# Normed expert results written as rows by indirect DMA, in a two-layer decoder step with grouped MoE

## The reference

```
x <- LN(a*x + mixer(x))                      # HGRN2 in layer 0, GLA in layer 1
x <- LN(a*x + memory_cross_attention(x))
x <- LN(a*x + grouped_moe(x))                # a = (2*DEPTH)**0.25
```

```
h = silu(x @ w_gate[e]) * (x @ w_up[e])      # 1024 -> 512
y = y + combine[..., e:e+1] * (h @ w_down[e])
mu = mean(z); var = mean((z - mu)**2); z = (z - mu) * rsqrt(var + 1e-5) * g + b
```

## Time and profile before

| what | us |
| --- | --- |
| median of 3 runs (1395.2 to 1398.28) | 1397.25 |
| the profiled execution | 1396.09 |
| its span | 1394.3 |
| PE busy / DVE / ACT / POOL | 1346.6 / 1023.6 / 756.0 / 140.6 |

### The profile page before, as it was taken

One profiled execution on the slowest core, in us unless ns is written; L12 is line 12 of the kernel. 1 busy time (PEld: TensorE's weight loads), 2 busy tenths in 40 slices (PEclk: granted clock), 3 DMA queues, 4 the chain that ended last, 5 costly groups with the idle time before them and its releaser, 6 DMA issues.

```text
span 1394.3 us, 19745 instructions
## 1 busy us (share of the span) xinstructions
PE 1346.6 (97%) x7689; PEld 1118.5 (80%) x7689; DVE 1023.6 (73%) x1102; ACT 756.0 (54%) x775; POOL 140.6 (10%) x209
## 2 busy tenths in 40 slices
PE   8999999999898999999999999999899999999996
PEld 6898997788676888888887798779777788888884
DVE  4456757773578988898887256782558889898986
ACT  4445624423425876767676353332434777677765
POOL 5200246100000000000000015200000000000000
PEclk9999999999999999999999999999999999999998
DMA  9774545437954999999994455444983799999981
GB/s 284 258 256 151 166 154 145 127 122 261 370 228 154 363 360 337 354 349 351 338 357 146 130 192 171 133 150 170 375 318 143 276 366 340 350 345 338 363 319 38
DMA packets 102002, 353.67 MB, mean 254 GB/s; under 512 B 6368, under 2 KB 32496, under 8 KB 72224
## 3 DMA queue, kind: packets, MB, share of 16 engines
q1 hardware_dynamic: 97056, 336.09, 67.0%
q0 software_dynamic: 4864, 16.45, 3.5%
HBM read 332.85 MB, written 19.67 MB: 253 GB/s over the span
## 4 chain that ended last, share of the span: by engine, by line
PE 80%; DVE 10%; ACT 4%; DMA 3%; issue 1%; SPq 1%; DVEq 0%; ACTq 0%
PE ps L1883 65%; DMA att_kt<-in_cache_mem_v 2%; PE ps L2253 1%; DMA raw<-in_xattn_w_kv 1%; PE ps L2463 1%; PE ps L2276 1%; DVE mix_s L1594 1%; PE ps L2264 1%; PE ps L1892 1%; DVE x L1314 1%; PE ps L1891 1%; DVE x L1311 1%; PE ps L1993 1%; DVE x L1277 1%; DVE stats L1290 1%
## 5 line engine op out<-in xcount | busy, mean ns | idle before, releaser
L1247 DVE TENSOR_TENSOR w_lo<-raw,w_hi 128x2048 fp32r<-128x2048 f32 x64 | 146.0, 2293 | 125.9 <-ACT w_hi L827 125.8
L1883 PE MATMUL ps<-w_hi,xt_hi 128*128 128x512 f32 x576 | 229.6, 399 | 5.9 <-DVE w_lo L1251 2.2
L1883 PE MATMUL ps<-w_hi,xt_lo 128*128 128x512 f32 x576 | 225.5, 392 | 0.0
L1883 PE MATMUL ps<-w_lo,xt_hi 128*128 128x512 f32 x512 | 200.4, 392 | 0.0
L827 ACT ACTIVATE w_hi<-raw 128x2048 fp32r<-128x2048 f32 x64 | 121.7, 1913 | 141.8 <-PE ps L1883 64.6
L1251 DVE TENSOR_TENSOR moe_lo<-moe_in_raw,w_hi 128x2048 fp32r<-128x2048 f32 x72 | 164.2, 2290 | 22.6 <-ACT w_hi L834 22.6
L1251 DVE TENSOR_TENSOR w_lo<-raw,w_hi 128x2048 fp32r<-128x2048 f32 x72 | 164.8, 2291 | 16.7 <-ACT w_hi L834 16.2
L834 ACT ACTIVATE w_hi<-moe_in_raw 128x2048 fp32r<-128x2048 f32 x72 | 138.1, 1918 | 56.5 <-PE ps L1883 56.5
L834 ACT ACTIVATE w_hi<-raw 128x2048 fp32r<-128x2048 f32 x72 | 137.5, 1913 | 14.8 <-PE ps L1883 14.8
L1883 PE MATMUL ps<-xt_hi,w_hi 128*128 128x320 f32 x448 | 138.7, 310 | 0.2
L1883 PE MATMUL ps<-xt_lo,w_hi 128*128 128x320 f32 x448 | 138.4, 309 | 0.0
(11 more groups left out here) (407 smaller groups left out, 2573.0 us busy)
## 6 DMA issues: line engine op xcount, KB each, us to landing
raw<-in_moe_w_gate SPq DMA_DIRECT2D x48, 1024.0 KB, 5.2
moe_in_raw<-in_moe_w_down SPq DMA_DIRECT2D x48, 1024.0 KB, 4.9
moe_in_raw<-in_moe_w_up SPq DMA_DIRECT2D x32, 1024.0 KB, 5.7
raw<-in_moe_w_up SPq DMA_DIRECT2D x32, 1024.0 KB, 5.9
raw<-in_hgrn_w_in SPq DMA_DIRECT2D x16, 1024.0 KB, 5.6
raw<-in_cache_mem_k SPq DMA_DIRECT2D x16, 1024.0 KB, 6.3
moe_in_raw<-in_moe_w_gate SPq DMA_DIRECT2D x16, 1024.0 KB, 6.1
raw<-in_moe_w_down SPq DMA_DIRECT2D x16, 1024.0 KB, 5.0
```

The lines of the kernel that those rows point to most:

```text
L1247: nc.vector.tensor_tensor(lo_at(slot_of(k)), raw_at(slot_of(k)), hi_at(hi_slot(k)).bitcast(F32), ALU.subtract).then_inc(w_low, 1)
L1883: ins = mm(out, lhs, rhs, start=start and n == 0, stop=stop and n == 2, skip_group_check=shared)
```

## The change

The result of a visit stays in slot order. `row_sum` (DVE) adds a times the gathered input (`xa`, a copy of `xg` made by POOL) to the sums in PSUM, at the start of the next visit. ACT makes the row sums at j = 1 (`row_sums`) and, at j = 8, loads the table with Ln and Exp, computes 1/sqrt(var), and loads silu's table again (`row_rstd`). DVE does the two passes of the norm at j = 8 and j = 10 (`row_gain`, `row_norm`). POOL writes the 128 rows to the table `x_next[l]` in DRAM by an indirect DMA (`scatter`), with row numbers `row_out`; slots without a token go to row 0, which nobody reads. `s`, `pt`, `y_hi`, `y_lo`, `pick_t`, the scaling of x in visit 0, `tile_sums` and `tile_scale` go. `pick` of the next visit is made at DVE's j = 14, `ix` comes behind chunk 15, and in visit 0 a task `own` (j = 5) makes the row numbers of that visit. Between the layers SP loads x from `x_next[0]` and PE turns it behind three half blocks of the memory projection; at the end SP copies `x_next[1]` to the outputs. The diff, cut:

```diff
-SIDE = {1: ("s", 0), 3: ("s", 1), 5: ("s", 2), 7: ("s", 3), 9: ("s", 4), 11: ("s", 5),
-        12: ("pt", 0), 14: ("ix", 0), 20: ("t", 0), 21: ("t", 1)}
+SIDE = {5: ("own", 0), 15: ("ix", 0), 20: ("t", 0), 21: ("t", 1)}
...
     n = KT // len(X_AFTER)
     return range(X_AFTER.index(db) * n, X_AFTER.index(db) * n + n) if db in X_AFTER else ()
+def norms(q):
+    return TILES * (q - q // 3)
 def ln_loaded(q):
...
...
         for part in range(2):
             sp.wait_ge(mem_in[part], 32)
             sp.dma_start(late_mem[part].bitcast(F32), mem_rows_kept[part]).then_inc(mem_in[part], 16)
+    if l == 1:
+        dense(done, done + NR + 2, groups)
+        sp.wait_ge(mo[0]["out"], groups * 16)
+        for t in range(TILES):
+            sp.dma_start(x[0:live(t), t, :], x_next[0][1 + t * P:1 + t * P + live(t), :]).then_inc(x_in, 16)
+        done += NR + 2
     dense(done, in_end(l), groups)
     sp.wait_ge(mx_scan, 8 * l + H)
...
...
         group(l, last, i if groups is None else groups + i, i % GROUPS, False)
     group(l, last, nl if groups is None else groups + nl, GROUPS - 1, False)
     groups = nl + 1 if groups is None else groups + nl + 1
-for t in range(TILES):
-    sp.wait_ge(ln_done, TILES * (3 * LAYERS - 1) + t + 1)
-    rows = a["y_prompt"][0, t * P:(t + 1) * P, :] if t < 2 else a["y_sample"].rearrange("b t c -> (b t) c")
-    sp.dma_start(rows, x[0:live(t), t, :]).then_inc(y_out, 16)
-sp.wait_ge(y_out, 16 * TILES)
+sp.wait_ge(mo[1]["out"], nl * 16 + 16)
+sp.dma_start(a["y_prompt"][0], x_next[1][1:1 + PROMPT, :]).then_inc(y_out, 16)
+sp.dma_start(a["y_sample"].rearrange("b t c -> (b t) c"), x_next[1][1 + PROMPT:1 + NT, :]).then_inc(y_out, 16)
+sp.wait_ge(y_out, 32)
 for par in range(2):
...
...
     def gather(i):
-        pool.wait_ge(s["read"], side_start(i) + (3 if isinstance(i, int) else 9))
+        pool.wait_ge(s["read"], side_start(i) + (3 if isinstance(i, int) else 2))
+        pool.wait_ge(s["xa"], i + 1)
         nc.gpsimd.sem_inc(x_go, 1)
         nc.gpsimd.indirect_dma_start(st_moe["xg"][:], None, x_rows_out[l][:, :],
                                      bass.IndirectOffsetOnAxis(ap=row_ix[:, 0:1], axis=0)).then_inc(s["xg_in"], 16)
+    def keep_rows(i):
+        if isinstance(i, int):
+            pool.wait_ge(s["read"], 2)
+        else:
+            pool.wait_ge(s["read"], side_start(i))
+            pool.wait_ge(s["z"], i * 3)
+        nc.gpsimd.sem_inc(x_go, 1)
+        nc.gpsimd.tensor_copy(st_moe["xa"][:], st_moe["xg"][:]).then_inc(s["xa"], 1)
+    def scatter(i):
+        pool.wait_ge(s["z"], i * 3 + 2)
+        nc.gpsimd.sem_inc(x_go, 1)
+        nc.gpsimd.indirect_dma_start(x_next[l][:, :], bass.IndirectOffsetOnAxis(ap=row_out[:, 0:1], axis=0),
+                                     x[:, 1, :], None).then_inc(s["out"], 16)
+    keep_rows(0)
     gather(0)
     pool.wait_ge(rt_n, l + 1)
     nl = pool.value_load(n_last[0:1, 0:1], min_val=3, max_val=11)
     with pool.Fori(1, nl) as i:
+        keep_rows(i)
+        scatter(i)
         gather(i)
+    keep_rows(nl)
+    scatter(nl)
+    scatter(nl + 1)
...
-    def sums_out(g):
-        act.wait_ge(w_used, at(base, g, GCH))
-        nc.scalar.activation(m["y_hi"][:].rearrange("p (a c) -> p a c", a=2), ps[:, 4:6, :], ACT.Copy).then_inc(s["yh"], 1)
+    def row_sums(i):
+        act.wait_ge(s["z"], i * 3)
+        nc.scalar.activation(m["aside"][:], x[:, 0, :], ACT.Copy, scale=-1.0 / D, accum_out=mean_var[:, 0, 0:1]).then_inc(s["zs"], 1)
+        act.wait_ge(s["zs"], i * 4)
+        nc.scalar.activation(m["aside"][:], x[:, 0, :], ACT.Square, bias=mean_var[:, 0, 0:1], accum_out=mean_var[:, 0, 1:2]).then_inc(s["zs"], 1)
+    def row_rstd(i):
+        act.wait_ge(s["zs"], i * 4 + 1)
+        nc.scalar.activation(rstd[:, 0:1], mean_var[:, 0, 1:2], ACT.Ln, bias=ln_eps[:, 0:1], scale=1.0 / D).then_inc(s["zs"], 1)
+        act.wait_ge(s["zs"], i * 4 + 2)
+        nc.scalar.activation(rstd[:, 0:1], rstd[:, 0:1], ACT.Exp, scale=-0.5).then_inc(s["zs"], 1)
     def visit(i, first, last_one):
         g = i if groups is None else groups + i
-        if not first:
-            sums_out(g)
         uses = side_order(first, last_one)
...
             for e in range(EPG):
...
             for k, (jj, what, n) in enumerate(uses):
                 if max(jj, 0) == j:
                     side(i, what, n, side_start(i) + k + 1)
-            if first and 4 <= j < 4 + TILES:
-                act.wait_ge(s["xl"], TILES)
-                act.wait_ge(ln_in, rows_kept(l))
-                nc.scalar.activation(x[:, j - 4, :], x[:, j - 4, :], ACT.Copy, scale=ALPHA).then_inc(s["scaled"], 1)
             if j + MH < GCH or not last_one:
                 split_expert(l, j + MH, g, False)
             elif l == 0 and j + MH - GCH < NH:
                 split_next(j + MH - GCH, g)
+            if not first and j == 1:
+                row_sums(i)
+            if not first and j == 8:
+                nc.scalar.preload_act_table_set("natural_log_exp_and_others")
+                row_rstd(i)
+                nc.scalar.preload_act_table_set("silu_and_others")
     for k, (what, n, bank) in enumerate((("g", 0, 7), ("g", 1, 6), ("t", 0, 2), ("t", 1, 3))):
-        side(0, what, n, SKIPPED + k + 1, bank)
+        side(0, what, n, k + 1, bank)
     base = CHUNKS0 if l == 0 else CHUNKS1
     visit(0, True, False)
...
...
         visit(i, False, False)
     visit(nl, False, True)
     groups = nl + 1 if groups is None else groups + nl + 1
-    sums_out(groups)
+    nc.scalar.preload_act_table_set("natural_log_exp_and_others")
+    row_sums(nl + 1)
+    row_rstd(nl + 1)
     def kv_block_out(db):
         par = db % 2
         block_out(db, groups, kv_staged(db), ps[:, 4 * par:4 * par + 2, :], ACT.Copy).then_inc(evac[par], 1)
...
-    def sums_out(i):
-        dve.wait_ge(s["yh"], i)
-        V_.tensor_tensor(m["y_lo"][:].rearrange("p (a c) -> p a c", a=2), ps[:, 4:6, :],
-                         m["y_hi"][:].rearrange("p (a c) -> p a c", a=2).bitcast(F32), ALU.subtract).then_inc(s["yl"], 1)
+    def rows_taken(i):
+        if not isinstance(i, int):
+            dve.wait_ge(s["out"], i * 16)
+        V_.tensor_copy(row_out[:], row_ix[:])
+    def next_pick(i, first):
+        dve.wait_ge(s["side"], side_start(i) + (2 if first else 1))
+        dve.wait_ge(s["p"], i * 2 + 2)
+        for t in range(TILES):
+            ins = V_.tensor_scalar(m["pick"][:, t, :], slot_no[:], u_slot[:, t:t + 1], None, ALU.is_equal)
+        ins.then_inc(s["p"], 1)
+        dve.wait_ge(s["p"], i * 2 + 3)
+        V_.tensor_scalar(u_slot[:], u_slot[:], -float(P), None, ALU.add).then_inc(s["p"], 1)
+    def row_sum(i, g):
+        dve.wait_ge(w_used, at(base, g, GCH))
+        dve.wait_ge(s["xa"], i)
+        V_.scalar_tensor_tensor(out=x[:, 0, :].rearrange("p (a c) -> p a c", a=2), in0=m["xa"][:].rearrange("p (a c) -> p a c", a=2),
+                                scalar=ALPHA, in1=ps[:, 4:6, :], op0=ALU.mult, op1=ALU.add).then_inc(s["z"], 1)
+    def row_gain(i):
+        dve.wait_ge(s["zs"], i * 4)
+        V_.scalar_tensor_tensor(out=x[:, 1, :], in0=x[:, 0, :], scalar=mean_var[:, 0, 0:1], in1=ln_gb[:, 0, :],
+                                op0=ALU.add, op1=ALU.mult).then_inc(s["z"], 1)
+    def row_norm(i):
+        dve.wait_ge(s["zs"], i * 4 + 3)
+        dve.wait_ge(s["z"], i * 3 + 1)
+        V_.scalar_tensor_tensor(out=x[:, 1, :], in0=x[:, 1, :], scalar=rstd[:, 0:1], in1=ln_gb[:, 1, :],
+                                op0=ALU.mult, op1=ALU.add).then_inc(s["z"], 1)
     def visit(i, first, last_one):
         g = i if groups is None else groups + i
         if not first:
-            sums_out(i)
+            row_sum(i, g)
         uses = side_order(first, last_one)
         for j in range(GCH):
             for e in range(EPG):
...
                 V_.tensor_tensor(m["ht_lo"][:, e % 2], ps[:, 6, :].rearrange("p (k s) -> p k s", k=4),
                                  m["ht_hi"][:, e % 2].bitcast(F32), ALU.subtract).then_inc(s["htl"], 1)
             for k, (jj, what, n) in enumerate(uses):
-                if max(jj, 0) == j and not (what == "pt" and last_one):
+                if max(jj, 0) == j:
                     side(i, what, n, side_start(i) + k + 1)
+            if j == PICK_AFTER:
+                rows_taken(i)
+                if not last_one:
+                    next_pick(i, first)
             if j + MH < GCH or not last_one:
                 split_expert(base + j + MH, j + MH, g)
             elif l == 0 and j + MH - GCH < NH:
                 split_next(j + MH - GCH, g)
+            if not first and j in NORM_AFTER:
+                (row_gain, row_norm)[NORM_AFTER.index(j)](i)
     split_expert(base + 1, 1, g0)
     for n in range(2):
-        side(-1, "t", n, SKIPPED + 3 + n, 2 + n)
+        side(-1, "t", n, 3 + n, 2 + n)
     link(V_.tensor_reduce(m["gm"][:], m["sel"][:], AX_X, ALU.max))
     first_of(m["r2"][:], m["sel"][:], m["gm"][:], e_rank[:], EXPERTS)
...
```

(64 more changed lines are left out.)

95 lines of the change are left out of this document (24 added, 71 removed).

## The result

The changed kernel takes 1403.29 us (median of 17 runs, 1396.24 to 1410.26) against 1396.98 for the kernel before on the same chip (17 runs, 1395.13 to 1398.37). The ratio is 1.0041, 95% interval 1.0026 to 1.0055: slower by 0.4%, where 1391.0 was forecast, and 1.3 us past the range's upper end. The runs lie 14 us apart where those of before lie 3 apart.

A forecast was written before the change was run, and what follows sets the result against it. TensorE, busy 97% of the span, was taken as the bound. Layers -6.0, between them -1.5 and tail +1.0 sum to -6.5 us, from the median of 1397.25 to 1390.75, say 1391; range 1384 to 1402.

The forecast's parts named there:

- PE's work removed: Each visit but the first: TensorE loses six row sums (2.8 us) and pick's transposes (0.33), together 3.13 us.
- The first visit: First visit of a layer: net +0.35 us of PE work and 0.2 late, +0.55 in all.
- The table switch: ScalarE at j = 8: two table loads, 1.30 us per switch without a drain; 3.1 us with Ln and Exp.
- Rival 2: ScalarE at j = 8: a table switch costs double, load plus drain; PE waits 5.5 us four times; 1404; chance 0.05.
- The place and mean size of the stall: Visits 1 and 2 of both layers: PE waits 2.9 us ahead of "ix", as DVE's pick queues behind the scatter.
- Rival 1: rows_taken in visits 1 and 2: scatter lands late, change slower from about 10 us; 1407 at 11; chance 0.16.
- What a stall costs: Visits 1 and 2 of a layer: only the wait charged, -3.13 + 2.92 = -0.2 us each.
- Last visits: Last visit of a layer: no pick, no "ix", scatter wait hidden up to a landing near 9.8; keeps -3.13 us.
- Between the layers: Stretch to the dense blocks: they start at 28.3 us against 30.2, -1.9, of which -1.5 is kept.
- The tail: End of the kernel: scatter lands in 6.0 us, then DRAM-to-DRAM copy; 19.3 us against 18.28, +1.0.
- Rival 4: Tail: DRAM to DRAM at half the rate, +5 us rather than +1; 1395; chance 0.24 including a landing near 9.4.
- rival 3: Visits: scatter lands by 6.0 us, DVE's own queue sets a stall of 1.6; -13 us, 1384; chance 0.10.

The follow-up runs named there:

- the run of 1399.17: Profiled run of the changed kernel in the main measurement, unaltered; 1399.17 us, where the median of 17 runs is 1403.29.
- the run of 1412.95: Changed kernel measured again, unaltered; its profiled and longest run, 1412.95 us; median of 9 runs 1405.82, ratio 1.0056 against the kernel before.

## Why the prediction was wrong

- **PE's work removed**, 3.13 us a visit: right, 3.28 measured in undisturbed visits. The first visit: +0.44 in both layers, forecast +0.55.
- **The table switch**: right. The load ends where Ln starts and the next begins 0.02 behind Exp, as ScalarE's timeline of after has it:

```profile
542.48 1.28 ACT L1233 ACT_TABLE_LOAD   x1
543.77 0.30 ACT L1206 ACTIVATE rstd<-mean_var,ln_eps 128x1 f32<-128x1 f32 x1
544.10 0.20 ACT L1208 ACTIVATE rstd<-rstd 128x1 f32<-128x1 f32 x1
544.32 1.28 ACT L1235 ACT_TABLE_LOAD   x1
545.61 1.92 ACT L874 ACTIVATE w_hi<-moe_in_raw 128x2048 fp32r<-128x2048 f32 x1
```

The Trainium skill (ScalarE: Activation LUTs, "What ACT_TABLE_LOAD costs") adds a drain of 1.38 us to each; this trace has none. Rival 2 is out.
- **The place and mean size of the stall**: right in the run of 1399.17. Forecast 2.9 us four times; measured 3.50, 2.48, 2.73 and 1.98, mean 2.67. In the run of 1412.95 the mean is 4.75, past the 4.5 that I had named as refuting, because scatters landed up to 11.7 us after issue where I took 8.3 from the gathers. The step from landing to wait was right: the landing less 5.4, as worked out, in all eight. Rival 1 (a landing past 10) thus holds in one of the two profiles, not as a fixed value.
- **What a stall costs**: wrong, and this is the step that failed: "PE waits 2.9 us", and so visits 1 and 2 at "-3.13 + 2.92 = -0.2 each". The sum charged the wait and not the clock behind it. In the profile of 1399.17 the extra busy time is 1.88, 1.90, 1.87 and 1.87 us (72.59 - 70.71 and so on), of which the restart is 0.27 (70.98 - 70.71, where the clock held) and the clock 1.6; in that of 1412.95 it is 2.45 to 3.79. With the restart taken off, the four come to 6.4 us in the first and 10.8 in the second, the whole forecast gain of 6.5 and more. Twelve dummy matmuls ahead of the waits take the slow matmuls away and 5.5 us off the four visits at like landings, 11 to 14 off the medians. In the stretch between the layers before, 2.1 us of PE idle stand beside a clock of 1.00, and I looked no further.
The Trainium skill (TensorE: Matmul & The Clock Gate, "HAM oscillation") describes a kernel in which a wait for a DMA in every stage makes the clock fall each time, so that the cost is paid in every stage instead of once. The rows above agree: all eight index waits of the two profiles, 1.98 to 6.29 us, had the lower clock behind them. It should have been a rival with a chance of its own.
- **Last visits**: -2.18 and -3.32, forecast -3.13; the first had a PE wait of 0.85 for hidden units, which I had excluded. (The 67.2 us that the prediction gives for a last visit counts from 663.00, 2.1 us behind cw.)
- **Between the layers**: forecast -1.5, measured +3.4. Row_sum (+1.56 after the last chunk), row_norm's end (+7.2) and the scatter's issue (+8.0) came as worked out, and it landed sooner, after 5.9 us. But x's loads, issued at 749.63, let PE go on at 758.78, 9.1 us instead of 5.4, beside the weight loads. The turns and the last chunk then took 10.6 instead of 7.9: the first matmuls behind this wait of 6.1 us ran at the lower clock, a second stall priced without it.
- **The tail**: forecast +1.0, measured -1.3. The scatter went out at +6.76 as forecast and landed in 3.3 us, not 6.0. Rival 4 (the tail takes the gain) is out; rival 3 (a landing by 6.0) was seen in no visit, the soonest being 7.2.

Sums for the profiled run: layer 0 +1.5 (forecast -3.0), between +3.4 (-1.5), layer 1 -1.0 (-3.0), tail -1.3 (+1.0), together +2.6 of the span's +2.8. Of the 9.3 us between -6.5 and +2.8 the clock behind the four index waits is 6.4 and the stretch between the layers 4.9; the tail gave 2.3 back, and that was luck, a landing of 3.3 us where I had taken 6.0. The median lies 4.1 above the profiled run; later landings and more falls, as in the profile of 1412.95, would do that, but no profile of a run near the median shows it.

## What to carry to other kernels

A short wait of TensorE in a loop is to be priced twice, the wait and the lower clock behind it, and a wait for a DMA whose landing varies is to be priced by its late landings. Put what the busiest engine needs next ahead of such a wait in the queue of the engine between: here a swap of two calls turned +0.4% into -0.4%, and the pick two steps earlier made it -0.9%. Where the wait can't be moved, dummy matmuls in it are worth trying; here twelve steadied the runs and six didn't. Moving a wait is no gain by itself: the one that came back behind the turns brought the lower clock with it and ate 2.5 of the 3 us won.
